# A four-layer model on one core: row statistics by a product of ones, a start in small parts from two queues, dummy products ahead, and the input's squares summed by VectorE

## The reference

```
y = x * rsqrt(mean(x * x, over 2048) + 1e-6) * g
```

## Time and profile before

| | |
|---|---|
| median of 3 runs | 3139.74 us (3137.65 to 3139.76) |
| the profiled execution | 3135.53 us, span 3133.7 us |
| TensorE busy | 3091.3 us, 99% of the span, 25140 products |
| VectorE / ScalarE / GpSimd busy | 1746.9 / 1393.5 / 132.5 us |
| mean granted TensorE clock | 0.997 |
| DMA | 534.91 MB, mean 171 GB/s |
| lines 977, 978, 979, mean of one | 287, 283, 283 ns |

### The profile page before, as it was taken

How to read it: one execution, slowest core, us unless ns; L and a number is a source line. 1 busy time by engine, 2 the same in 40 slices (tenths; PEclk the granted TensorE clock), 3 DMA queues, 4 the chain that set the end, 5 groups by cost and what they waited for, 6 DMA issues and landing times.

```text
span 3133.7 us, 56219 instructions
## 1 busy us (share of the span) xinstructions
PE 3091.3 (99%) x25140; PEld 3050.4 (97%) x25140; DVE 1746.9 (56%) x2067; ACT 1393.5 (44%) x1467; POOL 132.5 (4%) x134
## 2 busy tenths in 40 slices
PE   8999999999999999999999999999999999999998
PEld 8889999999999999999999999999999999999997
DVE  6665544444445557765554554456666665555554
ACT  5444433333333357754333333345455454444442
POOL 2000000000000011110000000002000000000001
PEclk9999999999999999999999999999999999999998
DMA  6324454444554554455555555554444445444443
GB/s 217 108 101 146 168 178 175 174 173 177 175 175 173 176 194 172 175 182 185 185 185 187 188 189 189 188 177 178 161 149 152 167 162 194 165 166 171 166 164 119
DMA packets 77313, 534.91 MB, mean 171 GB/s; under 512 B 8464, under 2 KB 10768, under 8 KB 14352
## 3 DMA queue, kind: packets, MB, share of 16 engines
q1 hardware_dynamic: 77072, 531.31, 47.7%
HBM read 529.18 MB, written 2.10 MB: 170 GB/s over the span
## 4 chain that ended last, share of the span: by engine, by line
PE 94%; issue 3%; DVE 1%; ACT 1%; POOL 0%; DMA 0%; DVEq 0%; SPq 0%; ACTq 0%; POOLq 0%
PE PB L977 28%; PE PB L979 28%; PE PB L978 28%; PE PB L972 2%; PE PB L974 2%; PE PB L973 2%; PE PB L1033 0%; PE PB L1073 0%; PE PB L1122 0%; PE PB L1123 0%; PE PB L1034 0%; PE PB L1105 0%; PE PB L1106 0%; POOL acct L2012 0%; PE PB L1113 0%
## 5 line engine op out<-in xcount | busy, mean ns | idle before, releaser
L1443 DVE TENSOR_TENSOR WLt<-raw,WHt 128x2048 fp32r<-128x2048 f32 (+2 forms) x504 | 1144.2, 2274 | 943.6 <-ACT WHt L1171 943.6
L1171 ACT ACTIVATE WHt<-raw 128x2048 fp32r<-128x2048 f32 (+2 forms) x504 | 955.5, 1897 | 1313.8 <-PE PB L979 1252.7
L977 PE MATMUL PB<-XHt,WHt 128*128 128x256 f32 (+1 forms) x5072 | 1453.5, 287 | 16.8 <-DVE XLt L1446 8.9
L979 PE MATMUL PB<-XHt,WLt 128*128 128x256 f32 (+1 forms) x5072 | 1437.5, 283 | 0.0
L978 PE MATMUL PB<-XLt,WHt 128*128 128x256 f32 (+1 forms) x5072 | 1436.8, 283 | 0.0
L977 PEld LDWEIGHTS PB<-XHt,WHt 128*128 128x128 f32 x5072 | 956.6, 189 | 22.6 <-DVE WLt L1443 10.8
L978 PEld LDWEIGHTS PB<-XLt,WHt 128*128 128x128 f32 x5072 | 956.9, 189 | 2.5 <-issue 1.4
L979 PEld LDWEIGHTS PB<-XHt,WLt 128*128 128x128 f32 x5072 | 955.7, 188 | 0.0
L977 PE MATMUL PB<-HHt,WHt 128*128 128x256 f32 (+1 forms) x2432 | 691.9, 284 | 1.7 <-DVE WLt L1443 0.6
L979 PE MATMUL PB<-HHt,WLt 128*128 128x256 f32 (+1 forms) x2432 | 689.0, 283 | 0.0
L978 PE MATMUL PB<-HLt,WHt 128*128 128x256 f32 (+1 forms) x2432 | 688.4, 283 | 0.0
(11 more groups left out here) (197 smaller groups left out, 1505.9 us busy)
## 6 DMA issues: line engine op xcount, KB each, us to landing
raw<-in_gu SPq DMA_DIRECT2D x176, 1024.0 KB, 4.8
raw<-in_dn SPq DMA_DIRECT2D x88, 1024.0 KB, 4.8
raw<-in_odd_in SPq DMA_DIRECT2D x64, 1024.0 KB, 4.8
raw<-in_even_in SPq DMA_DIRECT2D x52, 1024.0 KB, 4.9
raw<-in_lru_in SPq DMA_DIRECT2D x28, 1024.0 KB, 4.9
raw<-in_mla_o SPq DMA_DIRECT2D x16, 1024.0 KB, 4.9
raw<-in_lru_o SPq DMA_DIRECT2D x16, 1024.0 KB, 4.9
raw<-in_even_o SPq DMA_DIRECT2D x16, 1024.0 KB, 4.8
```

What stands on the lines that cost most here:

```text
L977: t.matmul(o, wh, ah, start=first, stop=False)
L979: m = t.matmul(o, wl, ah, start=False, stop=last)
L1171: a.activation(hi, r, ACT.Copy).then_inc(s_hi, 1)
L1443: v.tensor_tensor(lo, r, hi.bitcast(f32), sub).then_inc(s_lo, 1)
```

## The change

1. The statistics at mix0, norm_ffn0, norm_mix1, norm_ffn1 and the last norm lose their spread and become `row_stat`: TensorE multiplies a whole 128 x 128 block of ones by the squares, so that every row of the PSUM bank holds the sums; VectorE scales into `R`, ScalarE takes the root of `R`, VectorE the reciprocal of `R`. The norms q, kv, even, final and ln_odd keep the column form.
2. The start: the parameters and the input, in six parts, are issued by ScalarE; unit 0 comes in four pieces, and SP issues only weights. The constants and tables go behind reloads. The input's squares follow unit 0 in ScalarE's order, their sums follow unit 1 and are VectorE's, the row statistic follows unit 3.
3. Three products of a tile of ones, 128 x 512, run on TensorE before anything else.
4. The end: the last unit's products go tile by tile. The squares of tiles 12 to 15 are not added by GpSimd but go to four places of `E1` and `E2` and into the product of ones. VectorE does all four closing multiplications, and the stores are in order.

```diff
+H_PARTS = [(0, 1), (1, 2), (2, 4), (4, 8), (8, 12), (12, 16)]
+FIRST_PIECES = {0: (0, 0), 1: (0, 1), 2: (0, 2), 3: (0, 3), 4: (1, 0), 6: (1, 1), 9: (2, 0), 11: (2, 1)}
 def pieces(n):
-    return 2 if n < 3 else 1
+    return (4, 2, 2)[n] if n < 3 else 1
...
-    p.after(2, stats0)
-    p.after(3, lambda: spread_end("mix0", "R", 0))
+    p.after(0, lambda: p.step("h_squares"))
+    p.after(1, lambda: p.step("h_sums"))
+    p.after(3, stats0)
...
-    start_stats("norm_ffn0", 0)
+    start_rows("norm_ffn0", 0)
...
# SP
-            s.dma_start(par[:, :], A["par"]).then_inc(s_par, 16)
-            load(0, 0)
-            load_h(0)
...
-            load_h(3)
-            s.dma_start(cst[:, :], A["cst"]).then_inc(s_cst, 16)
-            s.dma_start(tab[:, 0:960], A["tabA"]).then_inc(s_tabA, 16)
-            s.dma_start(sml[0:64, 144:148], A["lams"]).then_inc(s_lam, 16)
+            for n in range(3):
+                for j in range(pieces(n)):
+                    load(n, j)
...
-                    for n in range(3):
-                        reload(n + NRAW)
+                    reload(NRAW)
+                    s.dma_start(cst[:, :], A["cst"]).then_inc(s_cst, 16)
+                    reload(NRAW + 1)
+                    s.dma_start(tab[:, 0:960], A["tabA"]).then_inc(s_tabA, 16)
+                    s.dma_start(sml[0:64, 144:148], A["lams"]).then_inc(s_lam, 16)
+                    reload(NRAW + 2)
...
# TensorE
+                order = [(k, ti) for k in range(nk) for ti in range(len(tiles))]
+                if n == NU - 1:
+                    order = sorted(order, key=lambda o: o[1])
...
+            def row_stat(name, which, t0, width, summed, extra):
+                bank = own("st", name)
+                o = bank[:, t0:T]
+                if which is None:
                     t.wait_ge(s_cst, 16)
                     t.wait_ge(*when("hsum", 3))
+                    for i in range(4):
+                        m = t.matmul(o, ones, hsq[0][:, i * T:(i + 1) * T], start=i == 0, stop=i == 3)
                 else:
                     t.wait_ge(*when(*summed))
+                    m = t.matmul(o, ones, acc[which][:, t0:T], start=True, stop=not extra)
+                for mt in extra:
+                    t.wait_ge(*when("sq", ("last", mt)))
+                    m = t.matmul(o, ones, last_sq(mt), start=False, stop=mt == extra[-1])
                 m.then_inc(sems["sum"], 1)
...
+            t.wait_ge(*when("warm"))
+            for _ in range(3):
+                t.matmul(PB[7][:, 0:512], sqt[:, 0:128], sqt[:, 0:512], start=True, stop=True)
...
# ScalarE
             def prologue():
+                a.dma_start(par[:, :], A["par"]).then_inc(s_par, 16)
+                for i, (k0, k1) in enumerate(H_PARTS):
+                    a.dma_start(ht[:, k0 * T:k1 * T], A["h0"][:, k0 * T:k1 * T]).then_inc(s_h[i], 16)
...
+            def h_squares():
+                for q in range(4):
+                    a.activation(hsq[q], ht[:, 4 * T * q:4 * T * (q + 1)], ACT.Square).then_inc(sems["hsq"], 1)
...
+                elif what == "row_stat":
+                    name, t0 = x[0], x[2]
+                    a.wait_ge(*when("out", "st", name))
+                    a.activation(R[:, t0:T], R[:, t0:T], ACT.Sqrt).then_inc(sems["root"], 1)
...
# VectorE
+                v.memset(sqt[:, 0:512], 1.0).then_inc(sems["set"], 1)
...
+            def row_stat(name, which, t0, width, summed, extra):
+                b = plan.bank["st", name][0]
+                v.wait_ge(*when("sum", name))
+                v.tensor_scalar(R[:, t0:T], PB[b][:, t0:T], 1.0 / width, 1e-6, mult, add).then_inc(s_bank[b], 1)
+                v.wait_ge(*when("root", name))
+                v.reciprocal(R[:, t0:T], R[:, t0:T]).then_inc(sems["rt"], 1)
...
             def finish():
-                for q in range(3):
+                for q in range(4):
```

More of the change, by code:

```diff
@@ L182, in make_plan @@
         p.mark("xl", "x", "mix0", k)
+    p.mark("set", "warm")
     for q in range(4):
@@ L199, in stat, with rows_of @@
             summed[which] = ("sum", name)
+    def rows_of(name, which, t0, width, extra=()):
+        p.take("st", name)
+        p.mark("sum", "sum", name)
+        p.give("st", name)
+        p.mark("root", "root", name)
+        p.mark("rt", "rows", name)
+        p.step("row_stat", name, which, t0, width, None if which is None else sq.open.get(which), extra)
+        if which is not None:
+            summed[which] = ("sum", name)
     def square(which, first, name, what):
@@ L394, in make_plan @@
     xfree = [None]
-    ffn0 = ffn(0, 0, "norm_ffn0", ("norm_mix1", lambda: finisher("norm_mix1", 0, xfree[0])), ("out", "sp", "norm_ffn0"))
-    start_stats("norm_mix1", 0)
+    ffn0 = ffn(0, 0, "norm_ffn0", ("norm_mix1", lambda: finisher("norm_mix1", 0, xfree[0])), ("rows", "norm_ffn0"))
+    start_rows("norm_mix1", 0)
     p.step("lru_start", ffn0)
@@ L477, in even_parts @@
         return x, q
-    ffn1 = ffn(1, M0, "norm_ffn1", ("ln_even", even_parts), ("out", "sp", "norm_ffn1"))
+    ffn1 = ffn(1, M0, "norm_ffn1", ("ln_even", even_parts), ("rows", "norm_ffn1"))
     def even_stats():
@@ L871, in arrived @@
         def arrived(n, j):
-            if n < 3 and j == 0:
-                return s_first[n], 16
+            if j < pieces(n) - 1:
+                return s_first[n, j], 16
             return s_raw[n % NRAW], 16 * (n // NRAW + 1)
@@ L1377, in _ @@
                     prologue()
+                elif what == "h_squares":
+                    h_squares()
                 elif what == "prepare":
@@ L1656, in xb_out @@
                 for i in range(2):
-                    scaled_out(xbp[:, i, 3:3 + T], g, i, ("out", "sp", "norm_mix1") if q == 0 else None)
+                    scaled_out(xbp[:, i, 3:3 + T], g, i, ("rows", "norm_mix1") if q == 0 else None)
             def conv(q):
@@ L1881, in finish @@
             def finish():
-                v.wait_ge(*when("out", "sp", "last"))
+                v.wait_ge(*when("rows", "last"))
                 v.wait_ge(*when("hf", 15))
-                for q in range(3):
+                for q in range(4):
                     hq = h[:, 4 * q:4 * q + 4, M0:T]
-                    v.tensor_tensor(hq, hq, R[:, M0:T].unsqueeze(1).to_broadcast([128, 4, NT]), mult).then_inc(sems["done_v"], 1)
+                    v.tensor_tensor(hq, hq, R[:, M0:T].unsqueeze(1).to_broadcast([128, 4, NT]), mult).then_inc(sems["done"], 1)
             for what, *x in plan.steps:
@@ L1893, in _ @@
                     prologue()
+                elif what == "h_sums":
+                    h_sums()
                 elif what == "prepare":
@@ L1897, in _ @@
                     stat(*x)
+                elif what == "row_stat":
+                    row_stat(*x)
                 elif what == "spread_start":
@@ L1903, in _ @@
                     g, i, at = x
-                    scaled_out(c_[at], g, i, ("out", "sp", "mix0") if at == 0 else None)
+                    scaled_out(c_[at], g, i, ("rows", "mix0") if at == 0 else None)
                 elif what == "rtq":
@@ L1999, in _ @@
             for what, *x in plan.steps:
-                if what == "prologue":
-                    for q in range(1, 4):
-                        g.wait_ge(*when("hsq", q))
-                        if q > 1:
-                            g.wait_ge(*when("hsum", q - 1))
-                        g.tensor_tensor(hsq[0], hsq[0], hsq[q], add).then_inc(sems["hsum"], 1)
-                elif what == "square" and x[2] is not None:
+                if what == "square" and x[2] is not None:
                     src, which, slot, name, _, before = x
```

101 lines of the change are left out of this document (44 added, 57 removed).

## The result

| | before | after |
|---|---|---|
| median of the runs side by side | 3138.69 us (3135.60 to 3139.76, 4 runs) | 3122.08 us (3121.76 to 3122.37, 4 runs) |
| ratio | | 0.9950, 95% interval 0.9934 to 0.9966 |
| the profiled execution | 3135.53, span 3133.7 | 3122.28, span 3120.5 |
| TensorE busy, products | 3091.3, 25140 | 3088.2, 25096 |
| mean granted TensorE clock | 0.997 | 0.998 |

The kernel is faster by 16.6 us, 0.53%. The forecast started from a first median of 3139.74 us. The two profiled executions differ by 13.2 us, which is the sum of the prediction. The other 3.4 us are the subject of what follows.

A forecast was written before the change was run, and what follows sets the result against it. TensorE, busy for 99% of the span, was taken as the bound. Start 5.8, middle 2.5 and tail 4.9 made 13.2 us, taken from a median of 3139.7 to give 3126.5 us, range 3122.7 to 3133.

The forecast's parts named there:

- the sum of the prediction: Whole kernel: 5.8 from the start, 2.5 from the middle stages and 4.9 from the tail, 13.2 us less.
- the last one: Profiled execution to median: the median of the runs is 4.2 us above the profiled time, before and after alike.
- the middle stages: norm_ffn0 and norm_mix1 save 1.07 us each and norm_ffn1 0.4, together 2.5 us of TensorE's own time.
- the tail: After the last layer product: R ready at T0 + 4.9, end at T0 + 13.4, a gain of 4.9 us.
- The start: Up to the second group: first product at 7.9 us, second group at 33.8 instead of 40.59, 5.8 us gained after the clock charge.
- the 1.0 charged for it: Start: 1.0 us allowed for the clock not fully carried by the dummies, between bounds of nothing and 2.6.
- the first rival: Start: clock not carried past the dummies (1.6 us more), or ScalarE's issues long (1.1 later); 3128.2 us, chance 0.20.
- the rival of the late feed: Units 3 and 4: feed falls behind, cover negative by a late load, some 6 us lost; 3132.5 us, chance 0.12.
- the slower one: Start: loads and ScalarE, not GpSimd, stretch VectorE, unit 4 comes some 18 us later; 3144 us, chance 0.03.
- the shift absorbed: After the start: a later wait doesn't move, so the 5.8 us don't reach the end; 3132.3 us, chance 0.04.
- The estimate of 2.2 us: Reciprocal over 256 columns on VectorE: 2.2 us by the skill's eight repeated divides, half a us longer than the slope's 1.7.

The follow-up runs named there:

- e5: The kernel before, unedited, run again for a second trace: 3138.05 us.
- e10: The kernel before with the row product at mix0 only, in place of its one-column products and spread: 3134.70 us, ratio 0.9994.
- e7: The changed kernel with the whole end of the kernel before (column statistic, spread, GpSimd's share of the closing, k before tile): 3127.63 us.
- e8: The changed kernel with the even stage's two statistics and both spreads one unit later: 3119.42 us.
- e4: The changed kernel with the three sums of the input's squares on GpSimd again, at their new place in the order: 3124.57 us.
- e6: The kernel before with the three sums moved from GpSimd to VectorE behind unit 3's low half, statistic left in place: 3140.45 us, ratio 1.0010.
- e9: The changed kernel with norm_ffn0, norm_mix1 and norm_ffn1 back to column statistic and spread: 3126.21 us.
- e11: The changed kernel with one of four closing products on GpSimd again and stores in the order 0, 1, 3, 2: 3124.27 us.
- e12: The changed kernel with parameters and input issued by SP among its weights, none by ScalarE, and the even stage's statistics a unit later: 3117.92 us.
- e2: The kernel before with only the memset of ones and three dummy products added ahead: 3138.44 us, ratio 1.0001.
- e3: The changed kernel with parameters and input issued by SP between its weight pieces, none by ScalarE: 3121.81 us.

## Why the prediction was right, and where it failed

**The step that failed** is the last one: "the median of the runs is 4.2 above it, and I move it by the same". That took the scatter of the kernel before, 3135.1 to 3140.2 us over all its runs, for an offset that both kernels share. It is a matter of which clock falls an execution has: the profiled execution of the kernel before, at the low end of the scatter, has none between its start and the tail, and the one of e5, 2.5 us longer, has two. The prediction had no term for a fall in the middle, and its range none for this step. After the change the median lies 0.2 us below the profiled time and four runs span 0.6 us. So the gain at the median is 13.25 + 3.16 + 0.20 = 16.6 us: the difference of the profiled executions, the 3.16 by which before's median beside it exceeded its profiled run, and after's 0.2. Of the miss of 4.4 us, 1.0 is the first median of before, which was 1.0 higher than the one side by side. The longer series of 15 runs put the kernel before at 3137.7 to 3138.2, so the offset is rather 2.2 to 2.7.

The change takes only one of the two falls away. After's profiled execution has the fall of the even stage (1.3 us), which before's had not, and so the 13.2 us understate what an execution without falls gains. The execution of e5, which at 3138.05 us lies near the medians of the kernel before, has that fall too and the one at mix0 (1.5 us). Together that is 2.8 us beyond 13.2, which fits the 2.4 to 2.9 that the longer series leaves. The sizes are from the traces; that the median execution is like e5 is argued, since only two executions of the kernel before were traced. That the row product at mix0 is what takes its fall away rests on e5, e10 and the count of traces, and e10's own times leave its size open. Why an execution falls or doesn't is not settled.

**The sum** of 13.2 us in the profiled executions is in part luck: the middle stages gave 2.0 us more than forecast, after's fall and 0.4 us of the earlier start lost by 67 us took 1.7 of it back, and the tail gave 0.5 less.

**The start**: 5.94 measured, 5.8 forecast, by other parts. The first product came at 8.14 (7.9), since ScalarE's issues took until 4.66 and the first rows of the input waited 0.23 for their DMA. The clock was carried whole, so the 1.0 charged for it was not due in this execution; a stall of 0.44 and the small gaps took the rest. In e7 and e8, with the same start, the clock fell in or right behind gaps of 2.1 and 2.2 us: the first rival does occur, in some executions. The feed kept up at units 3 and 4; the rival of the late feed is out, and so is the slower one, since VectorE kept its pace with loads at 417 to 420 GB/s between 12 and 20 us and GpSimd idle. e4 and e6 name the cause of the stretch. Nor was the shift absorbed: T0 moved by 8.81 us, the 5.94 and the 2.87.

**The middle stages** were mis-sized: 4.5 us by the landmarks of e9, not 2.5. The statistics are about as priced, the slightly quicker pace of the ffn0 stage is the rest, and its cause is open. The net of 2.87 between the second group and T0 is smaller because after's execution has the even stage's clock fall (1.3) and before's had not, and because 0.4 of the earlier start is lost again by 67 us.

**The tail**: R at T0 + 4.90 as forecast, with a reciprocal of 1.75 us (1.74 from the slope of the rows). The estimate of 2.2 us made from the Trainium skill, "VectorE: DVE Perf Modes", "First, the fixed hardware budget", is too long; the trace doesn't agree with it. The end was T0 + 13.9 instead of 13.4, so the term is 4.4, not 4.9: the first store was issued at T0 + 6.15 as forecast, and the end comes 7.7 us behind it, not 7.3. By e11 the share of GpSimd was worth 1.8 to 2.2 of it. Against the shorter old ends of e6 and e10 the new one gains only 3.5.

**What each part is worth**: row product at mix0 about 3.0 at the median (2.8 by the traces where the fall comes), VectorE's sums 2.5 in the changed kernel (e4) and less than nothing without the later statistic (e6), middle stages 4.1, the end 4.0 by the trace of e7 (5.5 at the median, other falls included), dummies 0.8, the second queue nothing. Measured on different bases and with about a us of doubt each, these don't add to a sum.

## What to carry to other kernels

Before a forecast is moved from the profiled execution to the median, compare the two: where a kernel's runs scatter by more than the effect that you are after, look at the granted clock in short windows of several executions, for the scatter may be time that the change takes away. Do the same for the profile after the change, before two single profiles are subtracted. One-column products together with short waits can count twice on a busy TensorE, by their time and by the clock behind them, so move a statistic until its sum is ready (e8, e12), or give it whole-width products (e10). Dummies ahead are worth what is left after the gap to the first real product and after the next stall of the feed, so shorten the gap first.

## What the hardware did that I had not expected

- The granted clock fell to its lower level while TensorE counted as busy: behind 24 one-column products (2.1 us) with real products on both sides in e5, 1.5 us lost, and behind a wait of 1.15 us with 8 of them in ten of twelve traces, 1.3 us lost. The 8 without the wait (e8, e12) and a wait of 1.8 us without such products (e10) did not bring it down; right behind a wait of 3.2 us in e2 it fell (28.5 us).
- The dummies' gain held over gaps of 0.51, 0.96, 1.44, 1.45 and 1.62 us (e12, e3, e9, e11, after) and was gone over 2.10, 2.19, 2.28 and 2.63 us (e7, e8, e4, e2). The moment at which the clock had come up does not separate them: 4.6 us in e3, 5.9 to 7.4 in the other four that held, 4.5 to 5.0 in those that did not.
- Before its first change the granted clock reads 1.00 while products go at half pace (1.00 in the earlier trace rows, 0.222 us each). Behind it the column and the pace agree where I compared them: 0.50 and 0.21 us for 256 columns in e5 at 2185.
- Some 6,300 products in a row ran 0.2% quicker with no edit to them, the same in eight traces of one form and six of the other.
